# Even layer's recurrence: the transposed block inverses up to 32 wide made by VectorE's turning of 32x32 blocks

## The reference

```python
def wkv7_scan(r, w, k, v, a, bb):
    ...
    def step(state, inp):
        r_t, w_t, k_t, v_t, a_t, b_t = inp
        sa = jnp.einsum("bhvk,bhk->bhv", state, a_t)
        state = state * w_t[:, :, None, :] + sa[..., None] * b_t[:, :, None, :] + v_t[..., None] * k_t[:, :, None, :]
        return state, jnp.einsum("bhvk,bhk->bhv", state, r_t)
```

## Time and profile before

| what | value |
|---|---|
| time, median of 3 runs | 2474.15 us (2472.14 to 2485.48) |
| the profiled execution's own time | 2473.39 us |
| its span | 2471.6 us |
| TensorE busy in the span | 2361.9 us (96%) |
| VectorE busy | 1378.1 us (56%) |
| the recurrence in the span | from 1665.75 to about 1747 us |

### The profile page before, as it was taken

One profiled execution on the slowest core, in us unless ns is written; L12 is line 12 of the kernel. 1 busy time (PEld: TensorE's weight loads), 2 busy tenths in 40 slices (PEclk: granted clock), 3 DMA queues, 4 the chain that ended last, 5 costly groups with the idle time before them and its releaser, 6 DMA issues.

```text
span 2471.6 us, 51044 instructions
## 1 busy us (share of the span) xinstructions
PE 2361.9 (96%) x20054; PEld 2269.2 (92%) x20054; DVE 1378.1 (56%) x2481; ACT 1350.9 (55%) x2347; POOL 2001.7 (81%) x2171
## 2 busy tenths in 40 slices
PE   9999999999999999999999998889899998898999
PEld 8989999999999889999999998787899998798999
DVE  7784432457726865433458646644545447864550
ACT  5545555556645545556457646552554546656553
POOL 8987668899989977679899988350579997586997
PEclk9999999999999999999999999999999999999999
DMA  7554544456655554445456765130246665343665
GB/s 210 148 148 117 147 126 143 126 163 179 181 170 163 143 142 135 123 137 151 137 165 194 222 187 133 56 106 8 69 140 193 190 178 137 94 137 103 188 191 159
DMA packets 692381, 360.77 MB, mean 146 GB/s; under 512 B 13776, under 2 KB 689968, under 8 KB 692144
## 3 DMA queue, kind: packets, MB, share of 16 engines
q1 hardware_dynamic: 689168, 350.15, 49.5%
q10 hardware_dynamic: 2976, 7.36, 1.0%
HBM read 349.72 MB, written 1.05 MB: 142 GB/s over the span
## 4 chain that ended last, share of the span: by engine, by line
PE 69%; DVE 13%; POOL 8%; ACT 5%; issue 3%; DMA 2%; SPq 0%; ACTq 0%; DVEq 0%; POOLq 0%
PE pb L281 68%; POOL wl L372 8%; ACT wh L359 1%; ACT pool L309 1%; DVE bx L3660 1%; DVE pool L3839 1%; DMA raw<-in_w_in 1%; DVE u2l L680 1%; PE pb L584 1%; DVE pool L1177 0%; DVE pool L1176 0%; DVE pool L3699 0%; ACT bx L309 0%; DMA raw<-in_ffn_w 0%; DVE pool L643 0%
## 5 line engine op out<-in xcount | busy, mean ns | idle before, releaser
L372 POOL TENSOR_TENSOR wl<-raw,wh 128x256 fp32r<-128x256 f32 (+1 forms) x2164 | 1995.9, 954 | 457.2 <-ACT wh L359 436.9
L359 ACT ACTIVATE wh<-raw 128x1024 fp32r<-128x1024 f32 (+2 forms) x669 | 690.5, 1034 | 456.9 <-PE pb L281 233.2
L281 PE MATMUL pb<-xh,wh 128*128 128x272 f32 (+2 forms) x3104 | 926.9, 299 | 13.5 <-POOL wl L372 2.9
L281 PE MATMUL pb<-xl,wh 128*128 128x272 f32 (+2 forms) x3104 | 889.3, 287 | 0.0
L281 PE MATMUL pb<-xh,wl 128*128 128x272 f32 (+2 forms) x3104 | 889.2, 286 | 0.0
L281 PEld LDWEIGHTS pb<-xh,wh 128*128 128x128 f32 x3104 | 590.8, 190 | 34.2 <-POOL wl L372 9.6
L281 PEld LDWEIGHTS pb<-xl,wh 128*128 128x128 f32 x3104 | 591.1, 190 | 2.2
L281 PEld LDWEIGHTS pb<-xh,wl 128*128 128x128 f32 x3104 | 590.5, 190 | 0.0
L281 PE MATMUL pb<-pool 64*64 64x64 f32 (+9 forms) x2944 | 224.8, 254 | 40.7 <-DVE pool L1190 8.2
L281 PE MATMUL pb<-u2h,wh 128*128 128x256 f32 x840 | 239.1, 285 | 3.4 <-DVE u2l L680 3.4
L281 PEld LDWEIGHTS pb<-pool 64*64 64x64 f32 (+4 forms) x2944 | 168.4, 144 | 75.4 <-DVE pool L1190 10.4
(11 more groups left out here) (428 smaller groups left out, 3640.1 us busy)
## 6 DMA issues: line engine op xcount, KB each, us to landing
raw<-in_w_in SPq DMA_DIRECT2D x208, 512.0 KB, 3.8
raw<-in_ffn_w SPq DMA_DIRECT2D x120, 512.0 KB, 4.0
raw<-in_w_ffn_in SPq DMA_DIRECT2D x88, 512.0 KB, 3.8
raw<-in_w_branch SPq DMA_DIRECT2D x48, 512.0 KB, 4.1
raw<-in_od_w_in SPq DMA_DIRECT2D x41, 512.0 KB, 3.8
raw<-in_w_ffn_out SPq DMA_DIRECT2D x32, 512.0 KB, 4.2
raw<-in_ev_w_in SPq DMA_DIRECT2D x20, 512.0 KB, 3.9
raw<-in_w_out SPq DMA_DIRECT2D x16, 512.0 KB, 4.1
```

What stands on the lines that cost most here:

```text
L281: return e.matmul(out, lhsT=l, rhs=r, start=a, stop=z, skip_group_check=True)
L359: E.e.activation(hi, src, ACT.Copy).then_inc(*sig("weight_hi", ("hi", g)))
L372: E.e.tensor_tensor(lo[:, s, :], src[:, s, :], hi[:, s, :].bitcast(F32), SUB).then_inc(*sig("weight_lo", *[("lo", g, i) for i in ks]))
```

## The change

Up to level 4 all blocks are at most 32 wide, and every 32x32 block of XT is the transposed block of XX at the same place. VectorE has an operation that turns each 32x32 block of a tile. After the change the products for XT are left out of `pe_xx` and of `pe_merge` at levels 1 to 4, and VectorE makes XT from XX with it: once for a whole tile of 512 columns in `v_first`, and for each half of 256 columns behind the two XX copies of a level. A new signal, `turned`, is what `pe_merge` waits for; `pe_yy` waits as before for `inv`, which is now given when XX is written. Level 5 makes XT by products and masked copies as before. The identities that were written into XTS ahead of the masked copies (lines 3338 and 3380) go, since the turning writes all of the tile.

```diff
--- before.py
+++ after.py
@@ -3066,8 +3066,7 @@
                 B = banks[XX_BANKS[c][q]]
                 for a in HALVES:
                     x, y = AR[r, j, c, 0, a], BT[r, j, c * P + a.start:c * P + a.stop]
-                    mm(e, B[a, j * 64:(j + 1) * 64], x, y, True, True)
-                    m = mm(e, B[a, NS + j * 64:NS + (j + 1) * 64], y, x, True, True)
+                    m = mm(e, B[a, j * 64:(j + 1) * 64], x, y, True, True)
                 if j == 3:
                     m.then_inc(*sig("rw_xx", ("xx_s", c, q)))
 
@@ -3076,9 +3075,10 @@
         for q in range(2):
             b = XX_BANKS[c][q]
             e.wait_ge(*at("xx_s", c, q))
-            e.copy_predicated(XX[:, q:8:2, :], mask4(0, True), eights(b))
-            m = e.copy_predicated(XT[:, q:8:2, :], mask4(0, False), second_eights(b))
+            m = e.copy_predicated(XX[:, q:8:2, :], mask4(0, True), eights(b))
         m.then_inc(*sig("rw_v", ("inv", c, 0, 0), ("inv", c, 1, 0)))
+        e.wait_ge(*at("inv", c, 1, 0))
+        e.transpose(XT, XX).then_inc(*sig("rw_v", ("turned", c, 0, 0), ("turned", c, 1, 0)))
 
 
 
@@ -3118,11 +3118,12 @@
         for q in range(2):
             e.wait_ge(*at("yy", c, lv, q))
             if lv < 6:
+                e.wait_ge(*at("turned", c, q, lv - 1))
                 for i in range(4):
                     hh = 4 * q + i
                     for a in HALVES:
-                        mm(e, banks[6 + q][a, NS + i * 64:NS + (i + 1) * 64], XT[a, hh, :], YY[a, hh, :], True, True)
-            for i in range(4):
+                        m = mm(e, banks[6 + q][a, NS + i * 64:NS + (i + 1) * 64], XT[a, hh, :], YY[a, hh, :], True, True)
+            for i in range(4 if lv > 4 else 0):
                 hh, o = 4 * q + i, slice(i * 64, (i + 1) * 64)
                 if lv == 6:
                     m = mm(e, banks[6 + q][lo, o], YY[hi, hh, :], XT[hi, hh, :], True, True)
@@ -3139,8 +3140,14 @@
             if lv == 6:
                 e.tensor_copy(XLS[c][HALVES[0], hs, :], eights(6 + q)[HALVES[0]]).then_inc(*sig("rw_v", ("inv", c, q, lv)))
                 continue
-            e.copy_predicated(XX[:, hs, :], mask4(lv, True), second_eights(6 + q))
-            e.copy_predicated(XT[:, hs, :], mask4(lv, False), eights(6 + q)).then_inc(*sig("rw_v", ("inv", c, q, lv)))
+            m = e.copy_predicated(XX[:, hs, :], mask4(lv, True), second_eights(6 + q))
+            if lv == 5:
+                m = e.copy_predicated(XT[:, hs, :], mask4(lv, False), eights(6 + q))
+            m.then_inc(*sig("rw_v", ("inv", c, q, lv)))
+        for q in range(2 if lv < 5 else 0):
+            hs = slice(4 * q, 4 * q + 4)
+            e.wait_ge(*at("inv", c, q, lv))
+            e.transpose(XT[:, hs, :], XX[:, hs, :]).then_inc(*sig("rw_v", ("turned", c, q, lv)))
 
 
 
@@ -3333,9 +3340,6 @@
                     *sig("rw_v", ("rw_gap",)))
             yield
         yield
-        e.wait_ge(*at("k_ms", 1))
-        for a in HALVES:
-            e.tensor_copy(XTS[1][a], eight_idents(a))
         yield
         yield
 
@@ -3376,8 +3380,6 @@
         e = E.e
         e.wait_ge(*at("rw_ar"))
         e.wait_ge(*at("m_out", 7))
-        for a in HALVES:
-            e.tensor_copy(XTS[0][a], eight_idents(a))
         e.memset(LRS[0][:, 0:4, :], 0.0).then_inc(*sig("rw_v", ("lr_first",)))
         e.wait_ge(*at("lr_first"))
         e.wait_ge(*at("idents"))
```

## The result

The changed kernel took 2458.66 us (median of 11 runs, 2450.75 to 2466.58) against 2472.58 for the kernel before (11 runs): ratio 0.9937, 95% interval 0.9921 to 0.9953. That is 0.63% faster, 13.9 us between the medians. The forecast of 2462.0 lies 3.3 us above it, and the range held it; but the likeliest of its three outcomes was "within 0.5%" (0.62), and the measured one was "faster by over 0.5%" (0.35). The interval's upper end, 0.9953, lies just beyond that bound (0.995), so even this outcome is not certain.

A forecast was written before the change was run, and what follows sets the result against it. TensorE's small products and two VectorE copies were taken to bound a recurrence level in turn. Terms 7.4 + 0.6 + 2.7 - 0.1 + 0.9 = 11.5 us off 2473.4 gave 2462 us, range 2458.5 to 2469.

The forecast's parts named there:

- Merge products and pe_xx: TensorE in the recurrence: 8 merges shed 32 records each, 7.4 us; pe_xx halves, 0.6 us in chunk 1.
- Rival (d): Small products don't get cheaper, something else paces the records: 2.7 us less gain, 2465; (b) or (d) together 0.22.
- The hand-over: Between levels, second-half YY products need XX alone: 0.34 us earlier at each of 8 hand-overs, 2.7 us.
- The turning: VectorE's 32x32 transposes: 0.43 us for 256 columns, 0.7 for 512, hidden except 0.1 us lost at chunk 0's level 2.
- Line 3338's copies: Two removed earlier copies, where VectorE afterwards waits for ScalarE: counted as nothing; without that cover another 0.8 us.
- The start: Chunk 0, VectorE the path: dropped identities gain 1.0 us (bounds 0 and 1.3), turning loses 0.1; net 0.9.
- The clock: TensorE's wait at the start shortens from 2.89 to about 2.6 us; clock fall left in, gain 0.
- rival (a): Shorter wait no longer drops the clock, 1.1 us, plus 0.3 from earliest memset: 12.9 gained, 2460.5; with beyond, chance 0.22.
- the bound of 12.4: About 0.5%, 12.4 us: what a measurement of this kernel can tell from no change.

The follow-up runs named there:

- the later YY: Changed kernel with the YY products waiting for the turning too: recurrence 78.11 us against 68.26; 2465.45 us, ratio 0.9974 to the kernel before.
- dummies: Ten thrown-away products in TensorE's wait at the start; added to the kernel before, recurrence 80.11 us, 0.97 less; also added to three edits of the changed kernel.
- the identities with dummies: Changed kernel with chunk 0's identity copies into XTS put back ahead of the memset, plus ten thrown-away products in TensorE's starting wait: recurrence 73.56 us.
- the second set: Changed kernel run again without edit: 2462.48 us (8 runs), ratio 0.9953 (0.9931 to 0.9974) to the kernel before.

## Why the prediction was right, and where it failed

**Merge products and pe_xx (7.4 + 0.6): right.** Kept and unread they cost 8.00 us; 0.93 a level. Rival (d) is out: fewer records are cheaper in full proportion.

**The hand-over (8 x 0.34 = 2.7): right.** With the products kept a level is 4.32 against 4.65, 0.33. TensorE goes on 0.08 us behind the merge's end. One detail was off: the chain now runs through the first half's copy, not the second's.

**The turning (0.43 and 0.7, nothing on the path): right.** 0.42 and 0.71. No merge waits for it. VectorE is late only at level 2 of chunk 0, where 0.1 had been charged. From the first XX copy of level 1 to that of level 3, which takes in `pe_xx(1)` and `v_first(1)`, it was 10.99 us before (1681.46 to 1692.45) and is 7.93 now (1691.87 to 1699.80): 3.06 gained, where the terms give 2 x (0.93 + 0.34) + 0.6 - 0.1 = 3.04. Chunk 0's level 3 takes 3.35, said to be 3.4. Line 3338's copies gave nothing that can be told from scatter: from the instruction of the first row to TensorE's first small product it is 64.48 to 65.91 us in three profiled executions of the kernel before and 64.47 to 65.15 in five of the changed one, 0.4 apart in the mean. The Trainium skill ("Vector Engine (DVE) Microarchitecture Reference", The reshape front-end and per-opcode configuration) has the transposing mode at one element per cycle per lane; twice the columns take 0.29 us more here (0.42 to 0.71), 1.1 ns a column, so the trace agrees as far as it goes: the time grows with the columns as in one pass over the data, but no row here shows VectorE's cycle.

**The start (0.9 net): under-sized.** The memset starts 1.30 earlier against TensorE's first product, the first XX copy 1.27: the upper bound of 0 to 1.3, where 1.0 was taken. The identities put back cost 1.33 with the clock held. The lower bound was ill reasoned: the idle time ahead of the memset stays (0.38, 0.47 before), and all of the gain is had nonetheless, since the identities' 1.29 went from ahead of it. Turning in place of copying costs 0.12 there (3.24 - 1.79 from the first XX copy to the first of line 3055, against 4.39 - 3.06). Net 1.15, 0.25 more than the sum had.

**The clock: the step that failed.** "I leave the fall in: 0." The fall was kept in all executions for a wait foreseen at 2.6 us; the wait is 2.31 or 2.32, in three of five profiled executions the fall isn't there, and each of these gains 1.0 more. They are rival (a)'s 12.9, given 0.22: 12.8 measured. With the fall in, the start agrees with the other terms: 8.0 + 2.7 - 0.1 + 1.15 = 11.75, and 81.05 - (68.26 + 0.98) = 11.8. So 11.5 became 11.8 by the start and, where the clock held, 12.8, and the bound of 12.4 lies between. An outcome that hung on so little should have been given nearly even chances.

The clock was mis-stated in the other direction too. In the two executions that have the fall at the start a second and third fall cost 3.7 and 3.5 us more, which no term had. Over the five, 1.0 us kept in three is worth 0.6 on the average, and 7.2 us lost in two costs 1.4: 11.8 + 0.6 - 1.4 = 11.0. So the clock makes the 12.8 of the executions in which it holds, but on the average it does not carry the gain beyond the bound.

The length of the wait alone does not decide whether the clock stays. It fell behind 1.71 us in one run; behind 2.31 or 2.32 it stayed up in three profiled executions and fell in three (two of the changed kernel, one with the later YY). Behind 2.89 to 3.80 it fell in every profiled execution that had no dummies, six of six. Shown is that the kernel before had the fall in all three of its own, that the changed kernel has it in part of its executions, and that it costs 1.0. What decides between executions with the same wait stays open.

**What the recurrence does not explain.** The late fall at 58 us was in no term. None of four profiled executions of the kernel before (one with dummies) had it, two of five of the changed kernel did, and so did three of nine of its edited versions (the later YY, the turnings three times, the identities with dummies); with so few it can't be told whether the change makes it likelier. Over the five the changed recurrence averages (68.26 + 68.26 + 68.27 + 72.95 + 72.69) / 5 = 70.1 us, a gain of 11.0, while the medians differ by 13.9 here and by 11.0 in the second set. Over all executions of the unchanged kernels, 55 of before and 22 of after, the means are 2475.2 and 2460.7, 14.5 apart, with an uncertainty of 2.5 from their spreads of 4.9 and 5.1. Less the 11.0 to 12.8 placed in the recurrence this leaves 1.7 to 3.5 us, at the edge of that uncertainty. The stages outside do not place it either: ahead of the recurrence the profiled executions take 1665.75 to 1676.30 us before and 1665.94 to 1678.81 after, behind it 719.7 to 724.8 and 716.7 to 721.2, and each kernel scatters by more than what is missing. It stays open whether it is chance.

## What to carry to other kernels

Products that only give a transposed copy can go to VectorE if blocks of 32x32 suffice. Here the products themselves were 8.0 us; another 2.7 came from asking what still has to wait for the transposed form: only the second product of a level (the merge), so the turning lies beside the first (YY). Put the turnings behind both halves' copies, and look for the one place where another piece of work stands in the same queue. When a sum lands near the line between two outcomes, work out the chances from the unsure terms' ends, and keep a clock fall open when its wait is shortened only in part.

## What the runs showed of the hardware

**Turning is as cheap as a masked copy.** 32x32 blocks of float32 from SBUF to SBUF: 0.42 us for 128x256, 0.71 us for 128x512, against 0.44 and 0.71 for the copies of the same sizes from PSUM under a mask. GpSimd stood still beside the 256-wide ones.

**The clock falls differently in executions of one program.** The changed kernel's recurrence repeats to 0.01 us while the clock holds (68.26, 68.26, 68.27) and jumps by 4.4 to 4.7 when it falls, behind waits that agree to 0.01 us.

**One VectorE instruction can take seven times its length while GpSimd works without a pause.** Two pieces of VectorE's timeline, the two subtractions of 128x1088 at line 1857, first of the kernel before and then of the changed one:

```profile
1163.46 3.07 DVE L1857 TENSOR_TENSOR xl<-pool,xh 128x1088 fp32r<-128x1088 f32 x2 [0.77 <-ACT xh L1851]
```

```profile
1163.61 10.82 DVE L1857 TENSOR_TENSOR xl<-pool,xh 128x1088 fp32r<-128x1088 f32 x2 [0.77 <-ACT xh L1851]
```

The change touches nothing there, yet 7.7 us are lost. The long one is 9.62 us, the shortest at this line 1.28. Between 1163.6 and 1172.0 GpSimd finishes or works on ten of its splitting instructions (line 372) in the kernel before and thirteen in the changed one, where it pauses at 1172.09; the long subtraction ends 1.1 us behind that. In the same profile of before it was another instruction's turn, beside twelve of those splitting instructions in a row:

```profile
2034.16 7.20 DVE L3528 TENSOR_SCALAR pbuf<-pbuf,vec 32x256 f32<-32x256 f32 x1
...
2032.82 8.39 POOL L372 TENSOR_TENSOR wl<-raw,wh 128x256 fp32r<-128x256 f32 x12
```

In the changed kernel's first profile that one took 0.94 us. Such stalls come and go between executions of both kernels; the one at line 1857 is there again in one later profile of each. The recurrence starts at 1678.8 in one profile and 1665.9 in another of the same kernel, and 7.8 of these 12.9 us are line 1857 (10.82 against 3.06), which is why single spans were not compared here. That GpSimd causes them is argued from the rows that lie side by side; no run took its work away.
